# A two-layer streaming encoder step on one core: low halves of the index queries ahead of the decay constants, and the last transposes of the Sample's selected units ahead of the next scores

## The reference, cut to what matters

```
def layer(x, p, conv_buf, h0, past, lam_init):
    xn = rmsnorm(x, p['norm_pre'])
    proj = jnp.einsum('bld,de->ble', xn, p['w_in'])
    (a_x, a_g, b_q, b_k, b_v, b_g, b_iq, b_ik, b_iw, c_q, c_k, c_v, c_g) = jnp.split(proj, offs, axis=-1)
    ...
    y_a = a_h * jax.nn.silu(a_g)          # a: decay a = exp(-8 r softplus(-lambda)), h_t = a h + u
    # B: score = sum_h w_h relu(q_idx k_idx), the 256 best keys per query, softmax over them
    # C: softmax(map 0) - lam * softmax(map 1), times v, per-head RMSNorm
    mix = jnp.einsum('ble,ed->bld', jnp.concatenate([y_a, y_b, y_c], axis=-1), p['w_out'])
    x = x + rmsnorm(mix, p['norm_post'])
```

## Time and profile before

| | us |
|---|---|
| median of 3 timed runs | 1584.02 (1580.79 to 1585.23) |
| the profiled execution | 1586.94 |
| its span, first to last instruction | 1585.2 |
| TensorE busy | 1523.2 (96%) |
| VectorE busy | 1140.4 (72%) |
| ScalarE busy | 648.3 (41%) |
| mean granted TensorE clock | 0.987 of full |

### The profile page before, as it was taken

The page is one execution under the profiler, slowest core; times in us unless marked ns, Lnnn a source line. Parts: engine busy times, 40 slices in busy tenths (PEclk is TensorE's granted clock), DMA queues, the critical chain, the costliest instruction groups (busy, mean ns, idle before and its releaser), DMA issues. The chain is left out here.

```text
span 1585.2 us, 21171 instructions
## 1 busy us (share of the span) xinstructions
PE 1523.2 (96%) x7264; PEld 1026.0 (65%) x7286; DVE 1140.4 (72%) x2482; ACT 648.3 (41%) x1270; POOL 371.5 (23%) x461
## 2 busy tenths in 40 slices
PE   7999999999999899999989999999999999999997
PEld 5566556678877665566556665566788766556664
DVE  5479979998966556666443799899989666565662
ACT  3385760219143333434314757402371433343341
POOL 2000341430001244332310004404200121434221
PEclk9999999999999999999999999999999999999999
DMA  5101001231015112120411200023210341112111
GB/s 189 57 13 42 27 27 27 79 99 49 27 50 207 67 34 67 43 68 11 170 60 57 27 27 27 27 50 97 80 54 1 116 144 66 51 56 68 41 35 40
DMA packets 73114, 98.16 MB, mean 62 GB/s; under 512 B 42736, under 2 KB 61680, under 8 KB 68656
## 3 DMA queue, kind: packets, MB, share of 16 engines
q1 hardware_dynamic: 73008, 96.80, 19.9%
HBM read 65.79 MB, written 18.14 MB: 53 GB/s over the span
## 5 line engine op out<-in xcount | busy, mean ns | idle before, releaser
L1810 PE MATMUL ps<-r_xn,r_w 128*128 128x384 f32 (+1 forms) x1728 | 563.7, 476 | 7.8 <-DVE r_xn L1453 2.7
L1810 PEld LDWEIGHTS ps<-r_xn,r_w 128*128 128x128 f32 x1728 | 325.5, 192 | 198.4 <-issue 24.9
L1556 DVE TENSOR_SCALAR_CACHE_REDUCE r_ix<-r_sc,smi 128x768 bf16<-128x768 f32 (+6 forms) x380 | 342.1, 963 | 2.2
L1344 ACT ACTIVATE r_sc<-ps,sm 128x1024 f32<-128x1024 f32 (+8 forms) x204 | 155.5, 765 | 225.8 <-DVE sm L1690 225.6
L1896 PE MATMUL ps<-r_w,r_xn 128*128 128x256 f32 x1024 | 224.0, 380 | 0.0
L1896 PEld LDWEIGHTS ps<-r_w,r_xn 128*128 128x128 f32 x1024 | 193.8, 190 | 26.8 <-issue 1.0
L1690 DVE TENSOR_REDUCE sm<-ps 128x1 f32<-128x1024 f32 (+8 forms) x204 | 156.2, 786 | 54.5 <-PE ps L1985 20.5
L2032 PEld LDWEIGHTS ps<-r_vg,r_w 128*128 128x128 f32 (+1 forms) x1168 | 147.6, 192 | 53.1 <-issue 33.5
L2032 PE MATMUL ps<-r_vg,r_w 128*128 128x64 f32 (+1 forms) x1168 | 148.3, 271 | 1.3 <-DVE r_w L678 1.2
L2077 PE MATMUL ps<-r_xn,r_ag 128*128 128x512 f32 x256 | 134.2, 623 | 2.6 <-ACT r_vg L1360 2.6
L2077 PE MATMUL ps<-r_xn,r_vg 128*128 128x512 f32 x256 | 131.0, 607 | 0.4 <-DMA r_xn<-w_out 0.2
(11 more groups left out here) (256 smaller groups left out, 1868.9 us busy)
## 6 DMA issues: line engine op xcount, KB each, us to landing
r_w<-w_in SPq DMA_DIRECT2D x24, 1024.0 KB, 5.0
r_xn<-w_out SPq DMA_DIRECT2D x4, 2048.0 KB, 7.5
y<-r_res SPq DMA_DIRECT2D x15, 512.0 KB, 2.9
r_vg<-x SPq DMA_DIRECT2D x8, 512.0 KB, 8.6
r_w<-w_in SPq DMA_DIRECT2D x16, 256.0 KB, 5.5
r_xn<-vcache SPq DMA_DIRECT2D x2, 2048.0 KB, 12.5
o_v<-r_vg SPq DMA_DIRECT2D x4, 1024.0 KB, 10.6
r_sc<-x SPq DMA_DIRECT2D x8, 512.0 KB, 4.6
```

The source lines that it names most:

```text
L1344: ins = nc.scalar.activation(ex[2 * (i % 2) + m][0:r, 0:w], on_slot(("qk", i, m), w, r), ACT.Exp, bias=negm[0:r, c:c + 1], accum_out=den[0 ...
L1556: ins = vec.tensor_scalar(unsel[t][0:rows(t), :], sc[t][0:rows(t), :], b, None, op, ALU.add, accum_out=cnt[0:rows(t), c:c + 1])
L1810: ins = nc.tensor.matmul(on_ring(key, cn), w[:, k, P * s:P * (s + 1)], xnT[:, k, c0:c0 + cn], start=(k == 0), stop=(k == KT - 1))
```

## The change

In the attention part the third group of transposes of the Sample's B units follows the second at once (`groups[1:]`), ahead of the division and of the next unit's scores. The C units of the Sample still keep theirs back. The new branches with `ahead` hold for orders in which two selected units follow a selected one; with this order of tiles they are not reached, since unit 10's next-but-one unit is a C unit. In the front part the loop that makes the low halves becomes a function `lows(first, last)`; the first four low halves are made ahead of the constants, the remaining two and the two of the index keys where the loop stood.

```
+EARLY_LOWS = 4
...
         elif t == SAMPLE:
-            steps += one[:-1] + rest + ytr + one[-1:] + own + rows_now + two[:-1]
-            steps += groups[:1] + two[-1:] + pv + groups[1:2] + div
-            rest = groups[2:]
+            ahead = []
+            if i + 2 < len(units) and maps_of(i + 1) == maps_of(i + 2) == 1:
+                ahead = scores(i + 2)[0]
+            early = i == FIRST[n]
+            steps += one[:-1] + ytr + ([] if early else one[-1:]) + own + rows_now + two[:-1]
...
+            else:
+                steps += groups[:1] + two[-1:] + pv + groups[1:] + div
...
         else:
-            steps += own + one[:-1] + rest + ytr + two[:-1] + take(i, 1) + groups[:1] + rows_now + one[-1:] + two[-1:]
+            steps += own + one[:-1] + ytr + two[:-1] + take(i, 1) + groups[:1] + rows_now + one[-1:] + two[-1:]
...
+                    def lows(first, last):
+
+                        for n in range(first, last):
+                            key = list(RINGJOB)[n]
+                            _, u, c, p = key
+                            dve.wait_ge(high_ready, n + 1)
+                            if u == "iq":
+                                c0, cn = TOKENS[p]
+                                drains_ring(vec.tensor_tensor(iq3[1][:, c, c0:c0 + cn], on_ring(key, cn),
+                                                              iq3[0][:, c, c0:c0 + cn].bitcast(f32), ALU.subtract), key)
...
+                    lows(0, EARLY_LOWS)
                     dve.wait_ge(lam_e, 1)
                     link(vec.tensor_tensor(lamp, lams[:, 3:4], lams[:, 2:3], ALU.subtract))
...
-                    for key in list(RINGJOB)[:2 * len(TOKENS) + 2]:
...
+                    lows(EARLY_LOWS, 2 * len(TOKENS) + 2)
```

More of the change, by code:

```diff
@@ L209, in schedule @@
         elif t == SAMPLE:
-            steps += one[:-1] + rest + ytr + one[-1:] + own + rows_now + two[:-1]
-            steps += groups[:1] + two[-1:] + pv + groups[1:2] + div
-            rest = groups[2:]
+            ahead = []
[3 more added lines that the diff above has]
+            steps += one[:-1] + ytr + ([] if early else one[-1:]) + own + rows_now + two[:-1]
+            if ahead and len(ahead) == 3:
+                steps += groups[:1] + (one[-1:] if early else []) + ahead[:1] + groups[1:2] + ahead[1:2] + groups[2:] + pv + ahead[2:] + div
+            elif ahead:
+                steps += groups[:1] + ahead[:1] + groups[1:2] + pv + groups[2:] + ahead[1:] + div
+            else:
+                steps += groups[:1] + two[-1:] + pv + groups[1:] + div
         elif plain:
@@ L216, in schedule @@
         else:
-            steps += own + one[:-1] + rest + ytr + two[:-1] + take(i, 1) + groups[:1] + rows_now + one[-1:] + two[-1:]
+            steps += own + one[:-1] + ytr + two[:-1] + take(i, 1) + groups[:1] + rows_now + one[-1:] + two[-1:]
             steps += ROWS_AT.get(i, [])
-            rest = []
             steps += take(i, quota - 1) + pv + div + groups[1:]
@@ L1455, in _ @@
                             scale_x(t + 1, t + 2, xt[t + 1])
+                    third = slice(64, 96)
+                    def lows(first, last):
[7 more added lines that the diff above has]
+                                                              iq3[0][:, c, c0:c0 + cn].bitcast(f32), ALU.subtract), key)
+                            else:
+                                cols = slice(2 * IKW * p, 2 * IKW * (p + 1))
+                                vec.tensor_copy(iks[DI:2 * DI, cols], iks[0:DI, cols].bitcast(f32))
+                                link(vec.tensor_tensor(iks[third, cols], ikf[0:DI, cols], iks[0:DI, cols].bitcast(f32),
+                                                       ALU.subtract))
+                                vec.tensor_copy(iks[96:P, cols], iks[third, cols].bitcast(f32)).then_inc(kn_low, 1)
+                    lows(0, EARLY_LOWS)
                     dve.wait_ge(lam_e, 1)
@@ L1481, in _ @@
                        .then_inc(kc_low, 1)
-                    third = slice(64, 96)
-                    n = 0
-                    for key in list(RINGJOB)[:2 * len(TOKENS) + 2]:
[L1486 to L1498, removed]
+                    lows(EARLY_LOWS, 2 * len(TOKENS) + 2)
                     for j in range(AJ):
```

## The result

The changed kernel takes 1564.93 us (median of four runs, 1560.01 to 1568.41); the kernel before took 1583.86 us beside it. The ratio is 0.9881 with a 95% interval of 0.985 to 0.9912, so the change is worth 18.9 us. The forecast was 1563.5 us.

The account below looks back on a forecast made before the run. The prediction took TensorE, busy 96% of the span, as the bound. Gains of 9.1 us (opening) and 11.6 us (transposes) sum to 20.7, giving 1563.5 us, with its own range 1560 to 1567 and a wider one of 1558 to 1573.

Parts of the forecast that it names:

- What bounds it: Whole kernel: TensorE, busy 96% of the span, bounds it; reordering reaches only its standstills and the slow matmuls behind them.
- Part one: Opening projections: early low halves remove the 2.60 and 2.55 us stalls and the slow clock behind them, 9.1 us in all.
- That is 1.96 us to be had if no stall comes first: Opening, per layer: 32 matmuls of 320 columns take 8.58 us at full clock instead of 10.54.
- the lower bound named: Opening: 5.15 us gained if the stalls go but the clock falls anyway.
- Handed on: Threshold search behind the opening: VectorE has slack, so the opening's whole gain reaches the end time.
- rival B: Search on VectorE ends last and gives back the opening's gain: 1572.4 us, chance 0.06.
- Part two: Behind the Sample's selected units: small transposes and their copies moved ahead gain 5.8 us per layer, 11.6 in all.
- 3.1 clock: Behind the Sample's selected units: 3.1 us of each layer's 5.8 us gain comes from matmuls returning to full clock.
- A: Behind the Sample's selected units the clock falls all the same, leaving 5.4 us there: 1569.5 us, chance 0.16.
- The witness against it: At 471.20 to 474.60 TensorE idles 1.25 us and no clock fall follows, so short stalls should keep the clock up.
- C: Only the opening's gain counts, since other waits end last where the small copy did: 1574.9 us, chance 0.06.
- D: Small transposes wait for VectorE's copy of four behind a row maximum, 4 x 3.6 us lost: 1589.3 us, chance 0.02.

Follow-up runs that it names:

- transposes only: The changed kernel without the early low halves, so only the small transposes of units 10 and 11 move ahead; 1568.3 us, ratio 0.9913.
- filler in the transitions: The kernel before, with three and four unread extra matmuls in TensorE's 2.07 and 2.65 us standstills behind the Sample's selected units; 1575.6 us, ratio 0.9952.
- unit 10 alone: The kernel before, with only unit 10's small transpose moved ahead of the next scores; 1577.89 us, ratio 0.9971.
- unit 11 alone: The kernel before, with only unit 11's small transpose moved ahead of the next scores; 1576.0 us, ratio 0.9954.
- opening only: The changed kernel with the attention order of before, so only the early low halves remain; 1578.14 us, ratio 0.9967.
- filler in all places: The kernel before, with unread extra matmuls in the opening's stall and in both standstills behind the Sample's selected units; 1575.3 us, ratio 0.9956.
- filler in the opening: The kernel before, with four unread 384-column matmuls in each layer's opening stall; 1582.28 us, ratio 0.9999.
- one early low half: The changed kernel with only the first low half, instead of four, ahead of the constants; 1564.92 us, ratio 0.9883.
- the change again: The changed kernel unaltered, in a second series beside the kernel before; 1562.78 us, ratio 0.9872.

## Why the prediction was right, and where its terms were off

**What bounds it.** Right. No work was removed, and the 19 us are idle time of TensorE (10.6) and slow matmuls behind it (the rest), about half and half.

**Part one.** In the place itself the profile agrees with the forecast to 0.03 us: 4.53 us against 4.56. VectorE's order (three low halves, idle, the fourth, the constants) came as worked out; the fifth low half at 47.64 held up nobody. The term that was mis-sized is "That is 1.96 us to be had if no stall comes first", twice: 3.9 us. The chip gave 5.2 us for part one (3.5 to 7.0), the lower bound named. Two things are shown. First, the sum charged a slow stretch to every such stall, since the trace of before had one behind both; over the five profiles with the opening of before (before, transposes only, filler in the transitions, unit 10 alone, unit 11 alone) it fell behind 6 of these 10 stalls. By that count the term is 2 x 0.6 x 1.7 = 2.0 us on the average, not 3.9. Second, even these 2.0 did not show, in the time or in the mean clock, in any of the three comparisons that try the opening by itself (opening only, filler there, filler in all places beside filler in the transitions). One interval alone hardly decides that (the opening alone gave 7.0 us at most, where 7.2 would be needed, and the filler 2.2 at most, where 2.0 would be); it is the three together, and a count of slow stretches that fell in neither of the first two and by only 0.3 in the third, that speak against it. The stretches at 838.57 and 846.29 suggest that some of them turn up at the next short wait; two of seven profiles are not enough for that, and where they go stays open.

**Handed on.** Right. VectorE's first row maximum behind the search came at 439.23 instead of 445.02, with the same idle time in front of it. The 5.79 us between them are, to 0.03, the opening's 4.53 and the 1.23 by which this execution was early already:

```profile
439.23 2.36 DVE L1703 TENSOR_REDUCE sm<-ps 128x1 f32<-128x1024 f32 x2 [1.53 <-PE ps L2005]
```

So rival B, the opening's gain given back at the search, is refuted.

**Part two.** The waits were right one by one, and so was the 5.8 us for a layer with the clock up (5.72 in layer 0). The measured 13.8 us (10.8 to 16.8) does not rule out the forecast of 11.6. Idle time was 5.4 as said; if a term was too small it is the clock, "3.1 clock" per layer, 6.2, where 13.8 - 5.4 = 8.4 were measured and the filler matmuls alone gave 7.6. It was read from one execution with two stretches of 3.41 us per transition. The profile of the opening alone has three such lengths in each layer (6.83 and 3.41 us, at 512.54 and 526.19, at 1290.78 and 1304.43), that of the filler in the opening two and three; so the three profiles with both long stalls have 4, 6 and 5, and the one read had the fewest. What the forecast had right is more: in the five profiles that have them (before, opening only, filler in the opening, unit 10 alone, unit 11 alone) a slow stretch began in each of the 16 long stalls of the transitions or within 2.1 us behind it, against 6 of 10 for the opening's stall of much the same length.

**Rivals.** A, the clock falls in part two all the same, happened in layer 1 of the first profile, in one of two layers of the kernel with one early low half, and in none of the four transitions of "the change again" and "transposes only": 2 of 8. The prediction gave it 0.16 for all; as a partial event it happens, and in the first profile it cost 18.23 - 15.10 = 3.1 us. The witness against it, was a poor one: there 1.25 us of idle time had no slow stretch behind it, and here 0.78 us had one twice. The run-to-run spread of 8 us goes with the clock: the fastest run of the changed kernel (1560.01) had a mean clock of 0.998 and the slowest (1568.41) 0.993. In which places the clock fell in the runs without a profile is not known. C, part two gives nothing, and D, slower, did not happen: VectorE took up the copy of four within 0.1 us of the transposes' end (509.01 against 508.31 + 0.66), and the wait is 0.78 all four times.

The Trainium skill's rule cited ahead of the result ("TensorE: Matmul & The Clock Gate", Part 1: the activity watch runs freely, so its decisions do not start with the kernel) fits these rows: the same stall of 2.6 us is followed by a slow stretch in 6 of 10 cases. The pair of rows that the prediction named for it, at the scores of tile 4, is weaker than it reads: in layer 0 the stretch begins at 707.25, behind a wait of 0.78 us for ScalarE that comes after those scores, and in layer 1 at 1488.90, at the end of the wait of 1.22 us in front of them.

**The errors cancelled.** Part one gave 3.9 us less than the forecast, clear of the noise, and part two 2.2 us more, within it; the sum, 20.7 forecast, was 18.9. The good figure owes something to that luck.

## What to carry to other kernels

Price a stall of TensorE twice, once as idle time and once as half of the slow stretch behind it, but weigh the second with how often it follows, counted over several executions or from the mean clock of the timed runs: in one place here it followed 16 of 16 stalls, in another 6 of 10, and there a single profile can show all of it or none. The idle part arrived in full here, where TensorE is the bound. Before moving instructions, filler matmuls in the stall tell, by the time end to end and not in the place, what of its price is clock; and where two engines meet through one PSUM bank, put the small copy that frees it directly behind the large one: 0.8 us of waiting in place of 2.1 and 2.7.

## What the runs showed of the hardware

- The number of slow stretches is a property of the run as much as of the kernel. The 48 runs of before have 5.5 to 13 of them and lie between 1579.55 and 1588.41 us; within every kernel but one (unit 11 alone, whose 6 runs have 5.5 to 7.4) the time rises with their number, by 0.8 to 1.6 us for one (1.1 for before).
- The clock fell to 1.2 GHz behind waits of only 0.74 to 0.78 us (838.57 and 846.29; 1281.77, 1292.70 and, with one early low half, 511.72), though most such waits are followed by no fall. The three stretches behind the short stalls of the transition were twice as long (6.83 us) as those behind 13 of the 16 long ones (3.41).
- The change leaves one such place alone: at the scores of tile 4, behind waits of 1.2 and 0.8 us, twelve of the 24 layers in the twelve profiles have a slow stretch of 3.41 to 10.24 us (before: 707.25 and 1488.90).
- Removing a slow stretch in one place did not lower the mean number of them in the run for the opening (10.3, 9.7 against 9.2), and did for the transitions (5.3 with filler, 3.8 with the transposes moved, against 9.2). Why the two differ was not settled.
